# A one-core transformer block kernel: the first norm split between two engines, silu by table, one weight slot rounded before the first shift, a later load

## The reference

```python
mod = jax.nn.silu(c) @ ada_w + ada_b                  # c: 1 x 1024, ada_w: 1024 x 6144
shift1, scale1, gate1, shift2, scale2, gate2 = split(mod, 6)
u = rms_norm(x, norm1_g) * (1 + scale1) + shift1      # x: 256 x 1024
z = u @ w_in                                          # then attention branches, MLP, second block
...
kv = rmsnorm(mem, mem_norm) @ w_kv                    # mem: 256 x 1024, used by a memory attention of block 2
```

## Time and profile before

| what | us |
|---|---|
| median of 3 runs | 1047.28 |
| lowest and highest of the 3 | 1046.67 and 1047.86 |
| span of the profiled execution, first to last instruction | 1048.2 |
| TensorE busy in that span | 1026.5 |
| VectorE busy | 804.9 |
| ScalarE busy | 615.5 |

### The profile page before, as it was taken

One profiled execution on the slowest core, in us unless ns is written; L12 is line 12 of the kernel. 1 busy time (PEld: TensorE's weight loads), 2 busy tenths in 40 slices (PEclk: granted clock), 3 DMA queues, 4 the chain that ended last, 5 costly groups with the idle time before them and its releaser, 6 DMA issues.

```text
span 1048.2 us, 18924 instructions
## 1 busy us (share of the span) xinstructions
PE 1026.5 (98%) x6894; PEld 933.6 (89%) x6894; DVE 804.9 (77%) x1478; ACT 615.5 (59%) x1145; POOL 49.0 (5%) x74
## 2 busy tenths in 40 slices
PE   6999999999999999999999999999999999999998
PEld 5998989998988888988888889899999998888887
DVE  6987988877988655498887868567777868888753
ACT  5478789445656445466564457695654466565532
POOL 1011100011100000000000010000000020000000
PEclk8999999999999999999999999999999999999999
DMA  9997755666866666566665555545444555666663
GB/s 363 397 352 279 244 196 172 202 223 216 311 206 185 191 190 186 173 196 188 191 191 186 180 178 162 160 146 163 135 121 142 162 161 184 195 185 192 189 186 116
DMA packets 58508, 209.46 MB, mean 200 GB/s; under 512 B 7056, under 2 KB 8464, under 8 KB 57913
## 3 DMA queue, kind: packets, MB, share of 16 engines
q1 hardware_dynamic: 52616, 185.24, 55.5%
q0 software_dynamic: 5808, 23.09, 6.3%
HBM read 205.14 MB, written 3.16 MB: 199 GB/s over the span
## 4 chain that ended last, share of the span: by engine, by line
PE 88%; DVE 7%; ACT 3%; DMA 1%; issue 1%; DVEq 0%; ACTq 0%; SPq 0%
PE bank L691 87%; DVE ring_rounded L1856 3%; ACT rounded_rounded L1406 1%; PE bank L1038 1%; DMA ring<-in_stream 1%; DMA x<-in_x_t 0%; DVE ada_ring L2175 0%; DVE ada_ring L1912 0%; DVE body L1893 0%; ACT u_rounded L1463 0%; DVE body L2084 0%; DVE body_rounded L1900 0%; ACT body L1565 0%; DVE kcat L1986 0%; DVE part L2408 0%
## 5 line engine op out<-in xcount | busy, mean ns | idle before, releaser
L691 PE MATMUL bank<-u_rounded,rounded_rounded 128*128 128x256 f32 (+1 forms) x2152 | 508.8, 329 | 3.8 <-DVE ring_rounded L1856 3.4
L1856 DVE TENSOR_TENSOR ring_rounded<-ring,rounded_rounded 128x1024 fp32r<-128x1024 f32 x326 | 396.9, 1225 | 121.7 <-ACT rounded_rounded L1406 109.4
L1406 ACT ACTIVATE rounded_rounded<-ring 128x1024 fp32r<-128x1024 f32 x326 | 342.0, 1054 | 110.6 <-PE bank L691 90.7
L691 PE MATMUL bank<-u_rounded,ring_rounded 128*128 128x256 f32 x1504 | 352.3, 282 | 0.0
L691 PEld LDWEIGHTS bank<-u_rounded,rounded_rounded 128*128 128x128 f32 x2152 | 334.8, 189 | 7.6 <-issue 4.2
L691 PE MATMUL bank<-body_rounded,rounded_rounded 128*128 128x256 f32 (+1 forms) x1296 | 322.3, 336 | 2.0 <-DVE body_rounded L2114 1.3
L691 PEld LDWEIGHTS bank<-u_rounded,ring_rounded 128*128 128x128 f32 x1504 | 284.4, 189 | 36.8
L691 PE MATMUL bank<-body_rounded,ring_rounded 128*128 128x256 f32 x952 | 217.5, 281 | 0.0
L691 PEld LDWEIGHTS bank<-body_rounded,rounded_rounded 128*128 128x128 f32 x1296 | 201.7, 189 | 4.1 <-DVE body_rounded L2114 1.7
L691 PEld LDWEIGHTS bank<-body_rounded,ring_rounded 128*128 128x128 f32 x952 | 179.1, 188 | 26.3
L1660 ACT ACTIVATE part<-bank 128x256 f32<-128x256 f32 x65 | 24.9, 383 | 79.2 <-PE bank L691 79.2
(11 more groups left out here) (269 smaller groups left out, 883.8 us busy)
## 6 DMA issues: line engine op xcount, KB each, us to landing
ring<-in_stream SPq DMA_DIRECT2D x328, 512.0 KB, 4.1
ada_ring<-in_ada POOLq DMA_DIRECT2D x32, 512.0 KB, 5.7
body<-in_ada SPq DMA_DIRECT2D x8, 512.0 KB, 8.5
ada_ring<-in_ada SPq DMA_DIRECT2D x6, 512.0 KB, 7.6
mem_parts_kept<-body_rounded POOLq DMA_DIRECT2D x2, 1024.0 KB, 5.7
body_rounded<-mem_parts_kept POOLq DMA_DIRECT2D x2, 1024.0 KB, 5.4
x<-in_x_t SPq DMA_DIRECT2D x2, 512.0 KB, 4.6
body<-in_mem_t SPq DMA_DIRECT2D x2, 512.0 KB, 6.2
```

Of the source, the lines that this page charges most:

```text
L691: return nc.tensor.matmul(out, lhs, rhs, start=start, stop=stop, skip_group_check=True)
L1406: a(R(slot_round(q)), slot_weights(n), ACT.Copy).then_inc(slot_rounded, 1)
L1856: v.tensor_tensor(R(w), w, R(slot_round(q)), ALU.subtract).then_inc(slot_split, 1)
```

## The change

1. Only four blocks of `x` are squared on ScalarE. VectorE squares the other four in one instruction, adds the halves (4 blocks to 4, then 2 to 2), and TensorE makes 2 products with ones in place of 8.
2. silu(c) is one ScalarE activation with a table of its own; Tanh and the product on VectorE go, and the factor in the sums becomes 1. The table loaded at the start is another one; the number of table loads is the same.
3. Before `u[0]` is shifted, ScalarE rounds slot 0 alone. The copy of the bias line and slot 1 come behind `u[0]`. Banks are claimed by TensorE where each is first used.
4. SP issues the load of `mem` at k = 6 in place of k = 4. All eight squares of `mem` come behind `u[7]` on ScalarE. A small scaling of biases on VectorE (`half_bias`) moves behind the loop over k.

```diff
@@ block.sync
-                if k == KD // 2:
+                if k == KD - 2:
                     for half, name in ((slice(0, 4), "mem"), (slice(4, 8), "mem_end")):
                         sp.dma_start(mem_n[:, half, :], mem_t[:, half, :]).then_inc(loaded[name], 16)
@@ block.tensor
-            sum_row("x_ss", ROW_X, merged)
+            ps = claim("x_ss")
+            pe.wait_ge(x_summed, 2)
+            mm(ps[:, 0:T], mat("ones"), merged[:, 0, :], True)
+            done(mm(ps[:, 0:T], mat("ones"), merged[:, 1, :], stop=True), "x_ss")
...
-            for n in FIRST_BANKS:
-                if opens(n):
+            def claim_first(k, n):
+                if k == 0 and opens(n):
                     claim(n)
@@ block.scalar
-            nc.scalar.preload_act_table_set("exp_and_others")
+            nc.scalar.preload_act_table_set("silu_and_others")
             act.wait_ge(loaded["x"], 16)
-            row_square(merged, x, lambda i: act.wait_ge(loaded["x_end"], 16) if i == KD // 2 else None)
+            for i in range(KD // 2):
+                a(merged[:, i, :], x[:, i, :], ACT.Square).then_inc(row_squares_ready, 1)
             act.wait_ge(loaded["c"], 16)
-            a(c_tanh, c_row, ACT.Tanh, scale=0.5).then_inc(c_tanh_ready, 1)
+            a(c_row, c_row, ACT.Silu).then_inc(c_ready, 1)
             nc.scalar.preload_act_table_set("natural_log_exp_and_others")
             act.wait_ge(loaded["cols"], 16)
             row_inv("x_ss", 0)
-            full(act, "bias")
-            free(a(bias_line, bank("bias")[0:8, :], ACT.Copy, scale=HD ** 0.5), "bias")
             for k in range(KD):
-                ahead(f"u{k}", 2)
+                ahead(f"u{k}", 2 if k else 1)
                 act.wait_ge(u_normed, ROW_X * KD + k + 1)
                 act.wait_ge(ada_summed, 2 * k + 2)
                 a(R(u[:, k, :]), u_lo[:, k, :], ACT.Identity, bias=mod[:, k:k + 1]).then_inc(u_rounded, 1)
-                if k >= KD // 2:
-                    for i in (2 * k - KD, 2 * k + 1 - KD):
-                        act.wait_ge(loaded["mem" if i < KD // 2 else "mem_end"], 16)
-                        a(mem_squares[:, i, :], mem_n[:, i, :], ACT.Square).then_inc(row_squares_ready, 1)
+                if k == 0:
+                    full(act, "bias")
+                    free(a(bias_line, bank("bias")[0:8, :], ACT.Copy, scale=HD ** 0.5), "bias")
+                    ahead("u0", 2)
+            for i in range(KD):
+                act.wait_ge(loaded["mem" if i < KD // 2 else "mem_end"], 16)
+                a(mem_squares[:, i, :], mem_n[:, i, :], ACT.Square).then_inc(row_squares_ready, 1)
@@ block.vector
-                v.tensor_tensor_reduce(out=w, in0=w, in1=c_row, scale=0.5, scalar=col("ada_b", at), op0=ALU.mult, op1=ALU.add,
+                v.tensor_tensor_reduce(out=w, in0=w, in1=c_row, scale=1.0, scalar=col("ada_b", at), op0=ALU.mult, op1=ALU.add,
...
+            dve.wait_ge(loaded["x_end"], 16)
+            v.tensor_tensor(merged[:, 4:8, :], x[:, 4:8, :], x[:, 4:8, :], ALU.mult).then_inc(row_squares_ready, KD // 2)
+            dve.wait_ge(row_squares_ready, (ROW_X + 1) * KD)
+            for i, n in enumerate((4, 2)):
+                v.tensor_tensor(merged[:, 0:n, :], merged[:, 0:n, :], merged[:, n:2 * n, :], ALU.add).then_inc(x_summed, 1)
+                dve.wait_ge(x_summed, i + 1)
             dve.wait_ge(loaded["cols"], 16)
-            v.tensor_scalar(half_bias[:, :], cols[:, AT["b_gate_2"]:AT["b_gate_2"] + 24], 0.5, None, ALU.mult).then_inc(half_bias_ready, 1)
-            dve.wait_ge(loaded["c"], 16)
-            dve.wait_ge(c_tanh_ready, 1)
-            step(v.scalar_tensor_tensor(out=c_row, in0=c_tanh, scalar=1.0, in1=c_row, op0=ALU.add, op1=ALU.mult))
+            dve.wait_ge(c_ready, 1)
```

More of the change, by code:

```diff
@@ L488, in build @@
         spare += [flat(pair_q[:, 4 * i:4 * i + 4, :]) for i in range(2)]
-        c_row, c_tanh = ada_acc[:, 0, :], ada_acc[:, 1, :]
+        c_row = ada_acc[:, 0, :]
         sg_stat = sb("sg_stat", [P, TT, 12])
@@ L504, in build @@
         stored = sem("stored")
-        c_tanh_ready = sem("c_tanh_ready")
+        c_ready, x_summed = sem("c_ready"), sem("x_summed")
         zeros_ready, lines_ready, sg_w_ready = sem("zeros_ready"), sem("lines_ready"), sem("sg_w_ready")
@@ L850, in sum_gathered @@
                 done(ins, name)
-            def sum_row(name, row, src):
-                ps = claim(name)
-                for i in range(KD):
-                    pe.wait_ge(row_squares_ready, row * KD + i + 1)
-                    ins = mm(ps[:, 0:T], mat("ones"), src[:, i, :], i == 0, i == KD - 1)
-                done(ins, name)
             u_parts, hidden_parts, mem_parts = (u, u_lo), (hidden, hidden_lo), (mem_hi, mem_lo)
             pe.wait_ge(ones_ready, 1)
-            sum_row("x_ss", ROW_X, merged)
+            ps = claim("x_ss")
+            pe.wait_ge(x_summed, 2)
+            mm(ps[:, 0:T], mat("ones"), merged[:, 0, :], True)
+            done(mm(ps[:, 0:T], mat("ones"), merged[:, 1, :], stop=True), "x_ss")
             pe.wait_ge(loaded["bias_in"], 32)
@@ L876, in first_tokens @@
                     at_t = slice(t * P, (t + 1) * P)
+                    claim_first(k, n)
                     mm(first[n], R(u[:, k, at_t]), w_hi, k == 0 and opens(n))
@@ L900, in _ @@
                 w_hi, w_lo = take(SLOT)
+                claim_first(k, "vsw0")
                 pe.wait_ge(u_ready, ROW_X * KD + k + 1)
@@ L915, in _ @@
                     at_a, at_b = slice(2 * i * P, (2 * i + 1) * P), slice((2 * i + 1) * P, (2 * i + 2) * P)
+                    claim_first(k, a)
                     ins = mm(first[a], w_hi[:, at_a], R(u[:, k, :]), k == 0)
@@ L1965, in _ @@
                     scaled(k + 1)
+            v.tensor_scalar(half_bias[:, :], cols[:, AT["b_gate_2"]:AT["b_gate_2"] + 24], 0.5, None, ALU.mult).then_inc(half_bias_ready, 1)
             dve.wait_ge(row_squares_ready, (ROW_MEM + 1) * KD)
```

## The result

| | median | lowest to highest | executions |
|---|---|---|---|
| before | 1047.59 | 1045.78 to 1050.58 | 20 |
| changed | 1050.12 | 1047.84 to 1051.74 | 20 |

The ratio, taken in rounds in which both ran, is 1.0017 [1.0009, 1.0025]: the changed kernel is slower by 0.9 to 2.6 us. I had forecast 1047.1, with 1048.6 as the upper end. The difference lies at the bound of 0.2% that was named as telling something from nothing, but the interval leaves out 1.

The account below looks back on a forecast made before the run. Slot 19's landing, from a full DMA queue, was taken to set TensorE's restart at 90.89, absorbing the start's 0.9 us gain. Span 1048.2 - 0.2 = 1048.0; the median, 0.9 below span, gives 1047.1; range 1045.4 to 1048.6.

Parts of the forecast that it names:

- The landing of slot 19 sets the end: Start stage: slot 19's landing at 68.55, not TensorE's pace, sets when TensorE goes on at 90.89.
- rival 2: ScalarE's squares of mem, slots and copies outrun 3.0 us of cover: 1048.6 or so; sign, no idle before slots 18, 19; chance 0.11.
- So the landings stay: Ring loads: slots 14 and 19 keep their landing times; slot 19 lands only 0.2 us sooner (0 to 0.5).
- the queue running dry: DMA between k = 4 and 6, without mem: 0.7 us lost from the queue per k, held to be covered.
- 3.0 us of cover: ScalarE's idle time before slots 18 and 19, 2.07 + 0.93, against 2.1 us of delay from the squares.
- The sum of squares: Start, first norm: four TensorE passes end at 11.5 against 11.76 for 16; 0.25 us won.
- silu worth nothing: Start: silu by table gains nothing by itself, as the second ada_w sum waits for a block landing at 11.2.
- Rival 1: The start's 0.9 us gain passes through, the line of transfers moving up with TensorE: 1046.4; chance 0.17.
- The start as a whole: TensorE's first product of slot 0 moves from 16.37 to about 15.45, 0.9 us won; bounds 0.4 to 1.6.
- TensorE's clock: Low clock under slot 0 at the start: products of k = 0 priced as before, though it might return later.
- rival 3: Clock fall at 256 to 260, worth 1.7 us: none gives 1045.4, chance 0.09; one more gives 1048.8, chance 0.04.
- Span against median: Base of the sum: the runs' median taken as 0.9 us below the profile's span of 1048.2.

Follow-up runs that it names:

- e13: e12 with parts 1 and 2 added (new first norm, silu by table): 1047.07 us, ratio 0.9986 to the kernel before.
- e15: e13 with ten more TensorE passes, into a bank nobody reads, ahead of the norm's 4 passes: 1046.74 us, ratio 0.9981 to before.
- e9: Changed kernel with parts 4 and 1 undone: 1046.76 us, ratio 0.9987 to the kernel before.
- e4: Kernel before with part 4 alone (mem loaded at k = 6, its eight squares behind u[7]): 1049.24 us, ratio 1.0010 to before.
- e3: Changed kernel with part 4 undone (load of mem at k = 4, squares two at a time): 1048.32 us, ratio 1.0005 to before.
- e5: Changed kernel with only the load of mem put back to k = 4, squares still behind u[7]: 1047.96 us, ratio 1.0005 to before.
- e16: e12 with mem loaded at k = 6 and its eight squares behind u[7]: 1047.90 us, ratio 1.0005 to the kernel before.
- e17: e12 with the eight squares of mem behind u[7] alone, load still at k = 3: 1045.63 us, ratio 0.9981 to before.
- e6: Kernel before with mem loaded at k = 3 in place of k = 4: 1047.28 us, ratio 0.9997 to before.
- e1: Kernel before, unchanged, run and profiled once more: 1047.49 us, ratio 0.9999.
- e18: e12 repeated: 1046.67 us, ratio 0.9989 to the kernel before.
- e11: Changed kernel with the 1 MB table of biases loaded behind GpSimd's next two ada_w blocks: 1048.94 us, ratio 1.0008 to before.
- e8: Kernel before with the 1 MB table of biases loaded behind GpSimd's next two ada_w blocks: 1045.94 us, ratio 0.9986 to before.
- e10: Kernel before with part 3 alone (order before u[0], banks claimed at first use): 1046.99 us, ratio 0.9983 to before.
- e14: e12 with part 2 alone added (silu by table): 1046.46 us, ratio 0.9985 to the kernel before.
- e7: Kernel before with each pair of ada_w loads from k = 4 on issued one k sooner: 1048.27 us, ratio 1.0001 to before.
- e12: Kernel before with part 3, mem loaded at k = 3 and the table of biases later: 1045.65 us, ratio 0.9978 to before.

## Why the prediction was wrong, by its own steps

**The landing of slot 19 sets the end: right of its rounding, and of its landing where nothing else holds ScalarE.** In the nine profiles in which slot 19 is rounded after 66.8 and no fall of the clock comes near 256, span less slot 19 is 977.9 to 978.5, while slot 19 itself moves over 3.4 us (66.87 to 70.28). Behind it the kernel is one rigid piece. The wait for `qa` that I expected to grow to 2 us is 1.2 in the second profile, as in the earlier trace rows, since TensorE is not ahead there, and 0.4 in the first. In the kernels that have slot 19 before 66 and no fall, the difference is 978.0 to 980.0: in most of them something else takes part of the gain (e13 has 980.0; e15, with 979.9, has a fall of the clock). In fourteen of the twenty profiles slot 19 is rounded 0.02 us after it has landed, in e13 0.23 after. The other five, all with the pile, are told under rival 2.

**"So the landings stay": the step that failed.** I had priced the queue running dry between k = 4 and k = 6 at 0.7 us lost per k and dismissed it, because slots 10 and 11 waited in the queue by more than that. That wait was not enough, and the queue grew thin. In the five profiles with the load at k = 6, 0.5 to 0.6 MB were asked for and not yet moved at the lowest point between 36 and 44; in the other fifteen 1.2 to 1.8. By the table's upper group, 13.97 to 14.03 MB were moved by 48 us in the three profiles with the load at k = 6, and 14.38 to 15.02 in the nine with the load sooner. Against those from before to e9, which leave all else of the queue as it was (14.45 on the mean), 0.44 MB is missing, at 417 GB/s 1.1 us. Slot 14 came at 55.03 to 55.67, in place of 52.88 to 54.71. In the lower group it is the same: 14.38 and 14.54 MB against 14.83 to 14.98, and slot 14 at 53.68 and 53.86 against 52.74 to 53.27. My own price of 0.7 us for each k, 1.4 for two, was of the right size for the landings; in time it came to 1 to 2.4 us (by the ratio of e4, and by e4, e3 and e5 at like clock), and to 2.4 per mille by e16 against e17. "The same bytes go ahead of slot 14" is true, and no comfort: bytes asked for late leave the queue thin first and then stand in the way (slot 14, asked for at 44.57 in the second profile, lands 11.1 us later, in before 9.6).

What misled me was the view. I read a DMA share of 1.0 as a full queue. The share stayed at 0.94 to 1.02 in the windows in which the rate was 343 to 371 GB/s. And the row that I had, 351 GB/s at a share of 0.96 in 32 to 38, already stood behind a thin queue (0.6 MB at 30 us): I took part of it for "slow transfers that stay". In e6, with the load at k = 3, it is gone (424 GB/s in 32 to 36, where e1 has 311). e6 had an early start, though; e13 and e18, with the load at k = 3 and a late one, have such a stretch sooner (331 and 343 GB/s in 28 to 32, behind 0.7 MB near 24).

**Rival 2, the pile on ScalarE: not the cause by itself, but the cover that I gave it was not there.** Its sign, no idle time before slots 18 and 19, is there in the first profile, e5, e11, e16 and e17. In these five ScalarE takes 11.8 us from the rounding of slot 14 to that of slot 18; without the pile it takes 10.0 to 10.2 where it has no wait (e1, e8, e10, e14, e15, e18). Slot 19 had landed 0.86, 0.45, 1.32, 1.08 and 0.97 us before ScalarE came to it. I had counted on 3.0 us of cover from a profile in which slot 18 landed at 66.54; in e1 it lands at 64.47, and the only cover is 1.78 before slot 19. That is as much as the pile takes, so e5 and e17 keep the pile and lose nothing. But when slot 14 lands late, the pile hands the delay on to slot 19, whether or not slot 19 itself is late: in e11 and e16 some 1.1 to 1.3 us of the rounding of slot 19 are the pile's. In the second profile and in e4 slot 19 waits for its own landing. How much of the loss would be left with a late load and no pile is not shown.

**The sum of squares: mis-sized.** I took 0.25 us won. Ln starts at 12.03 and 12.38 in the two profiles, where the working had about 11.6. The parts were right on VectorE (these are its rows in the first profile), apart from a start at 6.52 in place of 6.3:

```profile
6.52 1.23 DVE L1934 TENSOR_TENSOR body<-x 128x1024 f32<-128x1024 f32 x1 [5.44 <-DMA x<-in_x_t]
7.78 1.95 DVE L1937 TENSOR_TENSOR body<-body 128x1024 f32<-128x1024 f32 x2
```

What I missed is that 16 passes are in part a run-up: in each profiled execution with them the passes are 0.43 us apart at first and 0.22 later, from the 8th pass on in e1 (5.11 us in all) and from the 13th in the execution of the earlier trace rows (6.25). The profile that I had was one of the longer ones. Means of the first product of slot 0: 16.08 with the old norm and order (before, e1, e4, e6, e7, e8), 15.65 with the old norm and new order (e9, e10, e12, e14, e16, e17, e18), 15.92 with both new (both profiles of the changed kernel, e3, e5, e11, e13). So the order brings 0.43 on the mean, of 0.67 in my sum, and the norm costs 0.27 where I had a gain of 0.25. The start as a whole won 0.16, not 0.9.

**silu worth nothing: nothing speaks against it.** e14 beside e12 and e18: 0.9985 beside 0.9978 and 0.9989.

**Rival 1, the gain passes through: wrong for the changed kernel, as I said, but not in general.** In e10 nothing but the start moves, and 1.7 per mille come through, or 0.3 to 0.6 us at like clock.

**TensorE's clock.** The fall near 256 that I had as rival 3 comes in some executions of both kernels (9 of 20 runs of the changed kernel have a mean clock of 0.998, the others 1.000). It raises span less slot 19 from 978.2 to 979.5 to 980.3, so 1.3 to 2.1 us; I had 1.7. It isn't the loss: the 11 runs without it still have a median of 1049.36. The other clock term, which I left alone, is as large: whether the clock comes up under slot 0 or later moves slot 6's request by a us and slot 14 with it. Five of the changed kernel's 20 runs lie at 1047.84 to 1048.18, the rest from 1049.26 on; its first profile is of the one kind (slot 6 asked at 20.33), its second of the other (21.72). That these groups are the two starts is an inference from two profiles. A late start costs 1.5 us at slot 14 on the mean with the load at k = 6, and 1.0 to 1.3 with it at k = 4 or 3 (e7 left out, whose queue holds more).

The Trainium skill, "TensorE: Matmul & The Clock Gate", Part 1, says that how many products run at the low clock at a kernel's start differs from run to run of the same kernel. The traces agree: 6.25 and 5.11 us for the same 16 passes. It advises against fitting to one count; I worked from the one that I had.

**Span against median.** I went from the profile's 1048.2 to the runs by taking off 0.9. Time less span is 1.68 to 1.76 in every profiled execution since; by that the profile of before was an execution of some 1049.9 us, 2.3 above the median of its kernel, with both clock events against it. So the base of my sum was an execution of before that had a late start and a fall of the clock. The 0.9 that I took off tied its span to the median of the runs and hid both; that the base came out right was luck. From the median of before, my steps would have given 1047.4 and the same miss.

**What stays open:** how much of the late load's cost goes by way of the pile, why packets are slower behind a thin queue, how much part 1 costs by itself (nothing or 1.8 per mille), what takes the gain when slot 19 comes before 66, and why e8's and e17's runs fell so often into the 0.998 class.

## What to carry to other kernels

A DMA share of 1.0 does not say that transfers are queued; compare GB/s with the best window of the same kernel and with the bytes that the loop asks for in a period, and if the rate is below the best and near what is asked for, little is in store. In this kernel a large load that nobody needs yet was better asked for early: moved later it first left the queue thin and then stood in front of the slots that matter. An engine that works without a wait hands a late landing on to all that stands behind it, so the cover of moved work is to be read in more than one profile. Before a change of a few us is predicted from a single profile, take a second one of the same kernel: here two profiles of one file differed by more than the effect, at the start and in the clock.

## What the runs showed of the hardware

The clock column of the trace reads 1.00 until its first event, whatever the products do. In the changed kernel's first profile a pass of 256 columns of the norm is 0.51 us, and the column says 1.00; the four passes after the filler are 0.28 each. In the window of 14 to 20 it says 1.00 as well, though the same products of slot 0 are spaced 0.21 us at first and 0.12 later in the same trace. Durations, not the column, tell the clock of a start.

A short idle stretch can bring the clock down in one execution and not in another. Between 252 and 260 TensorE idles for 1.9 us in both profiles of the changed kernel, waiting for VectorE's rest of a slot. In the second the clock stays at 1.00. In the first it is 0.78 and 0.80 in two windows of 4 us:

```profile
252.00:256.00 4.00, 2.13 (x11) 2.07 (x11) 3.52 (x9) 3.97 (x6) 0.00 (x0) 0.78 0.19 75
256.00:260.00 4.00, 4.00 (x29) 4.00 (x29) 4.00 (x7) 0.73 (x1) 0.53 (x1) 0.80 0.44 147
```

In e1 the window that stands at 0.57 in the earlier trace rows is at full clock:

```profile
256.00:260.00 4.00, 4.00 (x36) 4.00 (x35) 4.00 (x9) 1.73 (x3) 0.53 (x1) 1.00 0.33 131
```

Five products whose result nobody reads, issued while TensorE waits for its first real work, brought the four passes behind them from 2.05 to 1.13 us.

The DMA engines can be busy all the time and move less. In 44 to 48 the second profile has a share of 0.94 and 378 packets, before 1.02 and 444; the packets of 4 KB take 178 and 161 ns on the mean.
